# End of the page loop in a hybrid mLSTM and MLA step: activations reloaded in eight pieces, first head's first block moved ahead of the values

## The reference, cut to what matters

```python
xn  = rmsnorm(x, g_attn_norm)
z   = einsum('bsd,de->bse', xn, w_in)            # q, k, v, o, gates, latents of both branches
# attention of a sample over its 1024 cached rows and its new ones (8 samples = 8 batches)
k   = qk_norm(concat(lat @ w_uk, k_rope))         # per head, from the cached latent rows
p   = softmax(where(mask, (q . k) * ATTN_SCALE, -inf))
o   = (p @ lat) @ w_uv                            # values are the latent rows themselves
# mLSTM branch, 8 heads: each head needs q, k (128 columns each), v, o (256 each) of z
```

## Time and profile before

| what | us |
|---|---|
| median of 3 runs | 2893.04 (2891.14 to 2893.79) |
| profiled execution | 2892.51 |
| its span, first to last instruction | 2890.6 |
| PE busy in the span | 2838.0 (98%) |
| DVE busy | 1495.8 (52%) |
| ACT busy | 1131.8 (39%) |
| mean granted clock of PE | 0.994 |
| wait of PE behind the last key matmul | 5.17 |
| `turn_out` starts | 1124.57 |
| next phase's first matmul | 1140.61 |

### The profile page before, as it was taken

The page is one execution under the profiler, slowest core; times in us unless marked ns, Lnnn a source line. Parts: engine busy times, 40 slices in busy tenths (PEclk is TensorE's granted clock), DMA queues, the critical chain, the costliest instruction groups (busy, mean ns, idle before and its releaser), DMA issues. The chain is left out here.

```text
span 2890.6 us, 50971 instructions
## 1 busy us (share of the span) xinstructions
PE 2838.0 (98%) x19086; PEld 2657.2 (92%) x19086; DVE 1495.8 (52%) x2297; ACT 1131.8 (39%) x1813; POOL 104.6 (4%) x346
## 2 busy tenths in 40 slices
PE   8998999999999998999999999999999999999999
PEld 7865898898898887999999999999999999999999
DVE  5465544444444433445454434445677754677644
ACT  5536332332333232444544333333444433444433
POOL 0100000000000000000000000002100000001000
PEclk9999999999999998999999999999999999999999
DMA  6624412112212204656666555556555556555564
GB/s 196 224 77 104 132 44 58 51 37 62 58 35 53 59 31 165 188 176 191 180 195 181 161 170 165 160 171 189 163 162 160 155 157 183 168 166 161 147 176 130
DMA packets 695531, 393.32 MB, mean 136 GB/s; under 512 B 65096, under 2 KB 675986, under 8 KB 694424
## 3 DMA queue, kind: packets, MB, share of 16 engines
q1 hardware_dynamic: 683160, 378.64, 44.9%
q10 hardware_dynamic: 11824, 11.50, 1.2%
q0 software_dynamic: 368, 0.81, 0.1%
HBM read 368.13 MB, written 22.75 MB: 135 GB/s over the span
## 5 line engine op out<-in xcount | busy, mean ns | idle before, releaser
L288 DVE TENSOR_TENSOR w_lo_b<-stage,w_hi_b 128x2048 fp32r<-128x2048 f32 (+1 forms) x289 | 619.0, 2142 | 411.0 <-ACT w_hi_b L281 410.8
L300 PE MATMUL bank<-xnH,w_hi_b 128*128 128x288 f32 x2784 | 756.8, 299 | 3.5 <-PEq L191 3.5
L301 PE MATMUL bank<-xnL,w_hi_b 128*128 128x288 f32 x2784 | 751.4, 297 | 0.0
L281 ACT ACTIVATE w_hi_b<-stage 128x2048 fp32r<-128x2048 f32 (+1 forms) x289 | 517.8, 1792 | 568.2 <-PE bank L305 535.4
L300 PEld LDWEIGHTS bank<-xnH,w_hi_b 128*128 128x128 f32 x2784 | 524.8, 188 | 13.4 <-issue 12.8
L301 PEld LDWEIGHTS bank<-xnL,w_hi_b 128*128 128x128 f32 x2784 | 524.4, 188 | 0.3
L1556 PE MATMUL bank<-ukH,latH 128*128 128x384 f32 (+2 forms) x1280 | 458.0, 358 | 5.0 <-DVE latL L1810 3.9
L1560 PE MATMUL bank<-ukL,latH 128*128 128x384 f32 (+2 forms) x1280 | 459.7, 359 | 0.0
L1561 PE MATMUL bank<-ukH,latL 128*128 128x384 f32 (+2 forms) x1280 | 454.0, 355 | 0.0
L305 PE MATMUL bank<-xnH,w_lo_b 128*128 128x288 f32 x2784 | 396.4, 295 | 0.0
L1817 DVE TENSOR_REDUCE rk<-sq_n 128x3 f32<-128x384 f32 (+1 forms) x320 | 182.1, 574 | 403.3 <-ACT sq_n L1720 403.3
(11 more groups left out here) (480 smaller groups left out, 2757.1 us busy)
## 6 DMA issues: line engine op xcount, KB each, us to landing
stage<-in_w_in_dram SPq DMA_DIRECT2D x88, 1024.0 KB, 5.2
stage<-in_w_up_dram SPq DMA_DIRECT2D x88, 1024.0 KB, 5.4
stage<-in_w_down_dram SPq DMA_DIRECT2D x64, 704.0 KB, 4.6
raw<-in_cache_kv_latent_dram SPq DMA_DIRECT2D x256, 64.0 KB, 1.8
latf<-in_cache_kv_latent_dram SPq DMA_DIRECT2D x64, 256.0 KB, 2.5
stage<-in_w_branch_a_dram SPq DMA_DIRECT2D x16, 1024.0 KB, 5.5
stage<-in_w_branch_b_dram SPq DMA_DIRECT2D x16, 1024.0 KB, 5.3
stage<-in_w_out_dram SPq DMA_DIRECT2D x16, 1024.0 KB, 5.6
```

Of the source, the lines that this page charges most:

```text
L281: act.activation(h, a, ACT.Copy).then_inc(w_hi, 1)
L288: dve.tensor_tensor(lo, a, h.bitcast(F32), ALU.subtract).then_inc(w_lo, 1)
L300: pe.matmul(out, hi, xH(k), start=first and k == 0, stop=False)
L301: pe.matmul(out, hi, xL(k), start=False, stop=False)
```

## The change

The reload of xn is cut along the 16 chunks into four parts, and each part is loaded for `xnH` and for `xnL` (eight transfers of 0.59 MB, high and low alternating), with one semaphore per part. PE goes through block N0 directly behind `spread`, waiting before chunks 0, 4, 8 and 12 for the part that they read; `values` and the denominators follow it. On ACT the high split of block N0 moves ahead of `exps`. DVE's order stays. The next phase waits for the four semaphores in place of the one.

```diff
@@ (ahead of the phase)
-        xn_back = lasting("xn_back")
+        XP = 4
+        xn_back = [lasting(f"xn_back{x}") for x in range(XP)]
+
+        def xn_load(sp, x):
+
+            part = slice(x * KC // XP, (x + 1) * KC // XP)
+            sp.dma_start(xnH[:, part].bitcast(F32), xnH_dram[:, part]).then_inc(xn_back[x], 16)
+            sp.dma_start(xnL[:, part].bitcast(F32), xnL_dram[:, part]).then_inc(xn_back[x], 16)
+
+        def xn_ready(pe, k):
+            if k % (KC // XP) == 0:
+                pe.wait_ge(xn_back[k * XP // KC], 32)
...
@@ (SP)
                     sp.wait_ge(n_k, KG * NPG * NB)
-                    sp.dma_start(xnH[:].bitcast(F32), xnH_dram).then_inc(xn_back, 16)
-                    sp.dma_start(xnL[:].bitcast(F32), xnL_dram).then_inc(xn_back, 16)
+                    for x in range(XP):
+                        xn_load(sp, x)
...
@@ (PE)
                     maxima(At(NB - 1))
                     spread(At(NB - 1))
+
+                    def first_block(n, ready=None):
+                        block(pe, At(n), At(n), lambda k: xnH[:, k, :], lambda k: xnL[:, k, :], ready=ready)
+                    pe.wait_ge(n_sq, KG * NPG * NB)
+                    first_block(N0, lambda k: xn_ready(pe, k))
                     values(At(NB - 1), 0, NJ, last=True)
                     last_denominators(At(NB - 1))
-
-                    def first_block(n):
-                        block(pe, At(n), At(n), lambda k: xnH[:, k, :], lambda k: xnL[:, k, :])
-                    pe.wait_ge(xn_back, 32)
-                    first_block(N0)
                     turn_out(At(NB - 1))
...
@@ (ACT)
+                    split_hi(act, At(N0))
                     exps(At(NB - 1))
-                    split_hi(act, At(N0))
                     split_hi(act, At(N0 + 1))
...
@@ (PE, next phase)
-                    pe.wait_ge(xn_back, 32)
+                    for x in range(XP):
+                        pe.wait_ge(xn_back[x], 32)
```

## The result

| kernel | median us | lowest to highest | runs |
|---|---|---|---|
| before | 2892.17 | 2888.94 to 2894.57 | 12 |
| changed | 2898.77 | 2893.44 to 2902.17 | 12 |

What follows compares the result with a forecast made beforehand. The prediction took PE, busy 2838.0 of 2890.6 us, to bound the kernel. Its terms, -1.7 + 4.0 - 2.2 + 1.2 = +1.3 us, gave a median of 2894.3 us, range 2890.8 to 2898.5.

Steps and rivals of the forecast that it cites:

- The wait for the exponentials, -1.7: Behind the spread, block N0 fills PE's idle time until the exponentials are done: 1.70 us go.
- The block runs into the reload, +4.0: Block N0, moved ahead, waits for xn pieces, the last landing at 1116.5; it occupies 10.4 us instead of 6.45.
- The values at the high clock, -2.2: The values, now behind block N0, run at the high clock: 4.73 us in place of 6.95.
- The cover of `ol`, +1.2: Before `turn_out`, block N0 no longer covers reciprocal and `ol`, so PE waits: 1.2 us added.
- The clock in the chopped block: In block N0's first pass, the last pair of pieces decides whatever the clock; no term in the sum.
- rival A: Clock does not rise in block N0 with its waits for pieces: +4.0, +6.2 or +7.7 us; chance 20%.
- Everything behind `turn_out` "shifts with it": Work behind `turn_out`, released by PE's `w_uv` product, keeps its order and comes 1.3 us later.
- Rival B: Last pair lands at 1114.6 and the barrier's low-clock stretch is not paid: -3.3 us, 2889.7; chance 15%.
- rival C: The eight xn transfers land in no order, near 1116.5, and block N0 starts cold: +6.6 us, 2899.6; chance 3%.

Runs made afterwards that it cites:

- the fastest one: Changed kernel with values and denominators inside block N0, `turn_out` before its second pass, transposes inside block N0 + 1, 36 useless matmuls in the first wait: 2884.17 us.

## Why the prediction was wrong

The forecast was a sum of five terms. The profile and the runs say of each:

- *The wait for the exponentials, -1.7*: right. It is gone, the high split was ready, and ACT had the exponentials done 12 us ahead of the values.
- *The block runs into the reload, +4.0*: the mechanism was right, the size 0.9 us low. PE waited 0, 1.50 and 1.41 us before chunks 4, 8 and 12, all within the bounds given. The last pair landed later than in my sum. The last piece of `xnL`:

```profile
1106.30 0.47 SPq L1374 DMA_DIRECT2D xnL<-xnL_scratch  x1
...
DMA to landing us min/median/max: 4.9/8.2/11.5
```

  That is 1117.8, 15.1 us after the first issue, where the two whole loads took 14.2. In the eight other traces with pieces and the new order it was 14.1 to 15.2, and in the run with PE's old order 13.6. So the pieces changed the transfer time by -0.6 to +1.0 us, inside the bounds of -1.9 and +1.5. Issuing the eight took SP 4.1 us (1102.71 to 1106.77), not 2.7; whether that is where the time went is not shown. The moment of chunk 12, 8.87 us after the spread, against 7.9, is this term's error, +0.9.
- *The values at the high clock, -2.2*: right, -2.4 in the trace.
- *The cover of `ol`, +1.2*: right. The wait is 1.11 us, 1.39 from the denominators' start.
- *The clock in the chopped block*, taken as no matter because "the last pair decides, whatever the clock": **this is the step that failed.** It holds for the first chunks, not for the chunks behind the last wait and the second pass, which the sum priced at the high level. There the low level cost 1.0 us over chunks 12 to 15 (2.09 against 1.1) and 1.7 over the second pass (3.82 against 2.08). This was rival A, given 20%, and its sign came true: the granted clock was 0.50 at 1117. Its path was another, though. A had the clock never rise; here it rose at 1113.3 and fell at 1116.7, and between the two PE was busy for 1.7 us. The reason against A, that PE would have worked 6.8 of 8.4 us by then, did not keep the clock up.
- *Everything behind `turn_out` "shifts with it"*: wrong too, and no rival named it. The `w_uv` product and `turn_out` cost 3.0 us more, at the low clock. In the kernel before, the 6.45 us of block N0 lay ahead of them; the change took that dense work away and put the wait of 1.11 us for `ol` there, close ahead of the 0.80 us for `olat` that had been there before. Filling this stretch alone brought 2.1 us in the median, filling the piece waits alone 1.1, both 4.4; which of the two weighs more, the intervals cannot tell.

The sum of the terms as measured, without the clock, is about +2, which the run with all waits filled shows (+1.9 in its trace, +2.2 in its median). Rival B did not come; rival C did not either, since the pieces landed in order and PE began the block 0.61 us after the spread. That the middle group of runs had one low stretch of the two is likely but not shown; only one execution of each kernel has a trace.

The Trainium skill describes the first of the two stretches: its page TensorE: Matmul & The Clock Gate ("HAM oscillation — how this bites in real kernels") describes bursts of matmuls between waits for DMA that send the clock back to its low level. I left it at the 20% of rival A since its waits are 3 to 5 us and mine under 2. The trace agrees with the pattern, at shorter waits than the page's: 1.50 and 1.41 us. By the Trainium skill's rate for a transfer of 1 MB alone (DMA: Bandwidth & Descriptors, "Bandwidth") I had estimated the last pair 1.7 us later than in my sum. The traces show 1.0 us at most, and in the run with PE's old order it landed 0.6 us earlier.

## What to carry to other kernels

When a block of matmuls is moved, ask not only what it runs into but what dense work it took away from its old neighbours: in these traces small matmuls and short waits of 0.8 to 1.5 us, close together, brought PE to 1.2 GHz for 3.4 to 6.8 us, and what followed cost up to 1.8 times as much. Cut a block where its operands are late and put other ready work into the gap, so that neither wait stands alone. Useless matmuls in a wait are a cheap test of whether the clock is the cause, and they may pay in the final kernel, though neither of the two gains here (0.9 and 1.0 us) is clear of the intervals.

## What the runs showed that was not expected

How short the waits were at which the clock fell. In the changed kernel the clock fell in the second of two such waits (1.50 and 1.41 us, with 1.3 us of matmuls between them); in the kernel before with its first wait filled it fell in a wait of 1.70 us, behind waits of 0.43 and 0.62 us with only the transpose and the spread between them. Yet in the kernel before PE stands still for 2.98 us at a later barrier (until 1926.57), and the clock is 1.00 all round it, while in the changed kernel the same wait of 2.98 us (until 1934.60) was followed by a fall to 0.50. So the length of one wait alone does not tell it; why the one gap was spared and the other not stays open. The row and the stretch of the kernel before, beside those at 1934.60 and 1936.00 of the changed one:

```profile
1926.57 0.38 PE L300 MATMUL bank<-haH,w_hi_b 128*128 128x288 f32 x1 [2.98 <-PEq L2413]
...
1926.00:1936.00 10.00, 9.43 (x71) 9.46 (x72) 3.34 (x4) 5.67 (x6) 1.12 (x1) 1.00 0.70 209
```

What the clock costs differs from run to run of the same kernel, and the order of the runs by mean clock suggests that it made up most of the spread: 8.7 us in the changed kernel (clock 0.991 to 0.995), 3.5 in the fastest one (2883.09 to 2886.54). A profile of one execution, here the slowest of 12, overstates or understates such a change; the medians of the runs had to carry the verdict.
